# Gate weights of experts 20 and 27 loaded in six and five transfers of spaced rows instead of one

## The chip, the cores and the metric

The kernel runs on one core of a Trainium2 chip. The metric is the time of one execution on the device, in microseconds (us). The time before is the median of three runs; beside it stands one profiled execution, whose trace is read here. "Us" with two decimals after a row is a time from the start of the span of that execution, or a duration.

## What is computed

The reference is one decoder block over 256 tokens of width 1024 with 16 meta tokens ahead of them: an RMSNorm, a combined input projection, a pooling mixer and a gated DeltaNet, an output projection, and then a mixture of 32 experts in four groups, of which each token uses the two best of its best group. The expert part is what matters here:

```python
for gi in range(N_EXPERT_GROUPS):
    hdn = (jax.nn.silu(jnp.einsum('nd,edf->nef', xt, w_gate[gi]))
           * jnp.einsum('nd,edf->nef', xt, w_up[gi]))
    hdn = hdn * comb[:, gi, :, None].astype(hdn.dtype)
    y = y + jnp.einsum('nef,efd->nd', hdn, w_down[gi])
```

`w_gate` and `w_up` of an expert are 1024x512 and `w_down` is 512x1024, in float32: 2 MiB each, 6 MiB for an expert, 192 MiB for all 32. They are read from HBM once.

## The kernel before, in words

The front half (mixers and output projection) takes the first 300 us or so. There the first expert's weights are loaded in twelve transfers of 32 rows (L768), between the tiles of the input projection, and expert 1's gate and up in four transfers of columns each (L792).

The back half goes through the experts e = 0 to 31 in order. For each, TensorE does gate (L2143, c = 0, 32 records of the trace), up (L2143 again, c = 1, 32 more), parts of the gather of the next group of four experts (L2075, only while e < 28), turns of the hidden state (L2175, L2181), every second expert the spreading of results to tokens (L2154), and down (L2199). VectorE multiplies gate and up (L1697); ScalarE takes the gate's bank with silu (L1076) and copies (L1081, L1092).

The weights lie in `ring`, nine places of 16 KiB in each of the 128 partitions: three matrices (gate c = 0, up c = 1, down c = 2) of three experts (`RINGS = 3`, expert e uses places of e % 3). One matrix is one transfer: `dst` is a place of the ring over all 128 partitions, `src` is a contiguous 2 MiB block of HBM whose 128 rows of 16 KiB go to one partition each. `load_chunk` issues it from SyncE's queue (SP), in the order gate, up, down, expert after expert. Before expert e's gate is loaded, SP waits until expert e - 3's gate has been used (semaphores `gate`, `up`, `y`); nothing else holds a load back. So up to nine loads are queued or under way. The last expert's up is cut into two transfers of columns and its down into four (L709), each with a semaphore of its own.

When a transfer is complete, its semaphore `w_land...` stands 16 higher; TensorE waits in `landed(e, c)` until the semaphore of the place has the count that all loads into the place up to this one add up to. A transfer more therefore needs a count of 16 more.

Of the kernel before, what the change touches and what calls it, by code (L numbers as in the profile page):

```python
# [40 lines left out]
P = 128  # L41
# [33 lines left out]
RINGS = 3  # L75
# [12 lines left out]
SEEDS_AT = {0: [2], 1: [3]}  # L88
FIRST_BANK = [5, 4, 7, 6]
YS = 2 * EXPERTS - 1  # L90
WARM = 16
BRIDGE = 4
KQV = 4
# [321 lines left out]
def uses(n, k, slots):  # L415

    return (n - k + slots - 1) // slots


def build_block(nc, x, meta_tokens, norm_mix_w, w_in, conv_w, pool_w, pool_scale, a_log, dt_bias, dn_norm_w,  # L420
# [3 lines left out]
    with ctx:  # L424
# [16 lines left out]
        S = Named()  # L441
# [259 lines left out]
        def load_chunk(eng, e, c):  # L701

            dst = ring[:, RING_AT[3 * (e % RINGS) + c], :]
            src = (gate_v, up_v, down_v)[c][e]
            if e == EXPERTS - 1 and c:
                parts, name = ((2, "last_up_land"), (4, "last_down_land"))[c - 1]
                dst2, src2 = (v.rearrange("p (s m) -> p s m", s=parts) for v in (dst, src))
                for n in range(parts):
                    eng.dma_start(dst2[:, n, :], src2[:, n, :]).then_inc(S(f"{name}{n}"), 16)  # L709
            else:  # L710
                eng.dma_start(dst, src).then_inc(S(f"w_land{3 * (e % RINGS) + c}"), 16)

# [18 lines left out]
        def _(sp):  # L731
# [28 lines left out]
            for step in SEQ_OF["sp"]:  # L760
# [32 lines left out]
                if step[0] == "early":  # L793
                    if step[1] == 0:
                        filled(sp, ("oT", HEADS - 1))
                    else:
                        low_made(sp, len(TILES) + KT - 1)
                        low_made(sp, len(TILES) + KT - 2)
                    load_chunk(sp, 2, step[1])
            sp.wait_ge(S("outproj"), 3)  # L800

            def one_pass(ps):
                base = EXPERTS * ps
                again = not isinstance(ps, int)
                for e in range(EXPERTS):
                    if e == RINGS and not again:

                        sp.wait_ge(S("logits"), TT)
                        sp.dma_start(wfin, norm_final_w[None, :].to_broadcast([P, D])).then_inc(S("wf_land"), 16)
                    for c, used in enumerate(("gate", "up", "y")):  # L810
                        if e >= RINGS:
                            sp.wait_ge(S(used), base + (e - RINGS + 1))
                        elif again:
                            sp.wait_ge(S(used), base)
                        if again or (e and (e, c) not in EARLY):
                            load_chunk(sp, e, c)
# [15 lines left out]
        def _(act):  # L832
# [231 lines left out]
            def one_pass(ps):  # L1064
# [3 lines left out]
                for e in range(EXPERTS):  # L1068
# [25 lines left out]
                    if g == 1 and not last:  # L1094

                        act.wait_ge(S("ysb"), YS * ps + 2 * e + 2)
                        act.wait_ge(S("give"), PAIRS * ps + (pair + 1))
# [670 lines left out]
        def _(pe):  # L1768
            T = nc.tensor
            pe.wait_ge(S("consts"), CONSTS["ones"])  # L1770
            for _ in range(WARM):
                T.matmul(pb[6][:, 384:384 + P], ones[:], ones[:], start=True, stop=True)
# [74 lines left out]
            for step in SEQ_OF["pe"]:  # L1847
                kind = step[0]
                if kind == "abp":
                    k = step[1]  # L1850
# [19 lines left out]
                if kind == "proj":  # L1870
                    n, k = step[1:]
# [72 lines left out]
                if kind == "sb":  # L1944
                    h, c = step[1:]
# [13 lines left out]
                if kind == "sa":  # L1959
                    h, c = step[1:]  # L1960
# [19 lines left out]
                if kind == "outk":  # L1980
                    k, i = step[1:]
# [5 lines left out]
                    for kk, half in which:  # L1987
                        if kk == 0:
                            bank(pe, ("out", 2 * i + half))
                        n = len(TILES) + kk  # L1990
# [30 lines left out]
            for n in range(TT * KT + 3):  # L2021
                if n >= 3:
                    cast_off(n - 3)
                if n < TT * KT:
                    k, i = n % KT, n // KT
# [34 lines left out]
            def one_pass(ps):  # L2060
# [49 lines left out]
                def landed(e, c):  # L2110

                    short = c and e % RINGS == (EXPERTS - 1) % RINGS
                    if e == 0 and not again:
                        pe.wait_ge(S(f"first_land{c}"), 4 * 16)
                        return
                    loads = ps * (uses(EXPERTS, e % RINGS, RINGS) - short) - (e % RINGS == 0)
                    quarters = QUARTERS - 1 if e % RINGS == 1 and c < 2 else 0
                    pe.wait_ge(S(f"w_land{3 * (e % RINGS) + c}"), 16 * (loads + quarters + (e // RINGS + 1)))

                def gate_up(e, c, name):  # L2120

                    q, j, i, g = e // 4, e % 4, e // 2, e % 2
                    first = e == 0 and not again
                    if not first and c == 0:
                        pe.wait_ge(S("xgT"), parts + PARTS * (q + 1) - 2)
                    if not (c == 1 and e == EXPERTS - 1):
                        landed(e, c)
                    if not first:
                        pe.wait_ge(S("hmid"), experts + e)
                        if c == 0:  # L2130
                            pe.wait_ge(S("hT"), experts + e)
                        elif g == 0:
                            pe.wait_ge(S("give"), pairs + i)
                    w = ring[:, RING_AT[3 * (e % RINGS) + c], :].rearrange("p (k q h j) -> p k h q j", k=KT, h=2, j=2)
                    for kt in range(KT):
                        if first and c == 0 and kt % 4 == 0:
                            pe.wait_ge(S("xgT_side"), kt // 4 * 2 + 2)
                        if first and c == 0 and kt % 4 == 2:
                            pe.wait_ge(S("xgT"), kt // 4 + 1)
                        if c == 1 and e == EXPERTS - 1 and kt % (KT // 2) == 0:  # L2140
                            pe.wait_ge(S(f"last_up_land{kt // (KT // 2)}"), 16 * ps + 16)
                        for half in range(2):
                            ins = T.matmul(pb[5 + c][half * 64:half * 64 + SLOTS, 0:256], xgT[:, q % ROOMS, kt, j * SLOTS:(j + 1) * SLOTS],  # L2143
                                           w[:, kt, half], start=(kt == 0), stop=(kt == KT - 1), skip_group_check=True)
                    ins.then_inc(S(name), 1)
# [12 lines left out]
                def spread_last():  # L2158

                    pe.wait_ge(S("give"), pairs + PAIRS)  # L2160
                    pe.wait_ge(S("ysb"), YS * (ps + 1))
                    for t in range(TT):
# [20 lines left out]
                def down(e):  # L2183

                    pe.wait_ge(S("hT"), experts + (e + 1))
                    if e == 0 and not again:
                        pe.wait_ge(S("most"), 1)
                    if again or e:
                        pe.wait_ge(S("ysb"), YS * ps + 2 * e)
                    if again and e == 0:  # L2190
                        pe.wait_ge(S("ysb_side"), 1 * ps)
                    if e < EXPERTS - 1:
                        landed(e, 2)
                    w = ring[:, RING_AT[3 * (e % RINGS) + 2], :].rearrange("p (j d) -> p j d", j=4)
                    for j in range(4):
                        if e == EXPERTS - 1:
                            pe.wait_ge(S(f"last_down_land{j}"), 16 * ps + 16)
                        for half in range(2):
                            ins = T.matmul(pb[7][half * 64:half * 64 + SLOTS, :], hT[:, j % 2, j // 2 * SLOTS:(j // 2 + 1) * SLOTS], w[:, j, half * 512:(half + 1) * 512],  # L2199
                                           start=(j == 0), stop=(j == 3), skip_group_check=True)  # L2200
                    ins.then_inc(S("y"), 1)
# [66 lines left out]
```

## Time and profile before

| | us |
|---|---|
| median of 3 runs | 781.25 (780.7 to 785.59) |
| the profiled execution, its own time | 781.17 |
| its span, first to last instruction | 779.4 |
| TensorE busy (749.0 us) | 96% of the span |
| DMA, mean over the span | 309 GB/s |

What lies between the span and the time of the profiled execution is 1.77 us. A busy TensorE says little by itself, since the ends of matmuls are modelled; which of TensorE's starts was held back by what is read from the waits, and how busy the 16 DMA engines were from the DMA share, the mean busy share of these engines.

### The profile page before, as it was taken

The numbers are of one execution on the slowest core, as the hardware profiler recorded it, in microseconds if no ns is written. First come the engines' busy times: TensorE is split into PE (matmuls) and PEld (weight loads), VectorE is DVE, ScalarE is ACT, GpSimd is POOL, SyncE is SP. The second block draws the span as 40 slices with busy tenths as digits, with TensorE's granted clock in tenths as the row PEclk, the third lists the DMA queues.
The fourth block names the chain that finished last, engine by engine and source line by source line (L and its number), as shares of the span: only waits on it lengthen the run. The fifth ranks groups of instructions, "written<-read, shape, count | busy, mean of one in ns | idle before, by whom it ended". The sixth has DMA issues, their size and how long they took to land.

```text
span 779.4 us, 16087 instructions
## 1 busy us (share of the span) xinstructions
PE 749.0 (96%) x6517; PEld 535.0 (69%) x6517; DVE 323.2 (41%) x794; ACT 312.1 (40%) x632; POOL 124.6 (16%) x208
## 2 busy tenths in 40 slices
PE   8999999999999999899999999999999988998895
PEld 7989989998999988655655555555556555455452
DVE  4784787688575855811311211221113112112012
ACT  6876678576684744712221221212122211111113
POOL 7473242225433640000000000000000000000000
PEclk9999999999999999999999999999999999999999
DMA  8537555564754568999999999999999999999992
GB/s 205 145 85 183 154 143 130 136 150 114 186 137 125 160 192 320 375 380 430 428 426 428 426 428 430 425 427 425 430 427 427 427 427 425 428 430 426 427 409 96
DMA packets 81104, 241.06 MB, mean 309 GB/s; under 512 B 6913, under 2 KB 65394, under 8 KB 68994
## 3 DMA queue, kind: packets, MB, share of 16 engines
q1 hardware_dynamic: 80722, 239.19, 80.7%
q8 instruction: 54, 0.88, 0.5%
q10 hardware_dynamic: 304, 0.79, 0.4%
q14 instruction: 24, 0.20, 0.1%
HBM read 238.92 MB, written 1.05 MB: 308 GB/s over the span
## 4 chain that ended last, share of the span: by engine, by line
PE 75%; DMA 11%; DVE 6%; issue 5%; POOL 2%; ACT 1%; DVEq 0%; POOLq 0%; ACTq 0%
PE banks L2143 23%; PE banks L1798 18%; PE banks L2199 12%; DMA ring<-in_expert_w_up_dram 10%; PE banks L2075 3%; PE banks L2154 3%; PE banks L1993 2%; PE banks L2175 1%; DVE desk L1367 1%; PE banks L1930 1%; PE banks L1917 1%; DVE rounded L1316 1%; PE banks L1934 1%; PE banks L1955 1%; PE banks L1978 1%
## 5 line engine op out<-in xcount | busy, mean ns | idle before, releaser
L2143 PE MATMUL banks<-ring,bench 128*64 128x256 f32 x2048 | 240.0, 388 | 11.6 <-DMA ring<-in_expert_w_up_dram 7.7
L2143 PEld LDWEIGHTS banks<-ring,bench 128*64 128x64 f32 x2048 | 146.2, 134 | 112.8 <-issue 23.1
L1798 PE MATMUL banks<-rounded 128*128 128x256 f32 (+3 forms) x1344 | 197.5, 293 | 1.4 <-DVE rounded L1328 1.0
L1798 PEld LDWEIGHTS banks<-rounded 128*128 128x128 f32 (+1 forms) x1344 | 170.1, 187 | 5.4 <-POOL rounded L1192 1.2
L1697 DVE TENSOR_TENSOR bench<-banks,bench 128x256 f32<-128x256 f32 x32 | 13.6, 425 | 263.0 <-PE banks L2143 172.1
L2199 PE MATMUL banks<-ring,bench 128*64 128x512 f32 x512 | 116.9, 598 | 0.5 <-ACT bench L1081 0.5
L1092 ACT ACTIVATE ysb<-banks 64x512 f32<-64x512 f32 x63 | 37.2, 591 | 147.1 <-PE banks L2199 146.3
L2199 PEld LDWEIGHTS banks<-ring,bench 128*64 128x64 f32 x512 | 33.9, 136 | 63.2 <-issue 60.1
L860 ACT ACTIVATE rounded<-room 128x1024 fp32r<-128x1024 f32 x64 | 67.4, 1054 | 22.5 <-PE banks L1798 15.0
L1081 ACT ACTIVATE bench<-banks 128x256 f32<-128x256 f32 x32 | 12.3, 384 | 148.1 <-PE banks L2175 148.1
L1316 DVE TENSOR_TENSOR rounded<-room,rounded 128x1024 fp32r<-128x1024 f32 x49 | 61.2, 1249 | 15.4 <-ACT rounded L860 14.3
L1185 POOL TENSOR_TENSOR rounded<-room,rounded 128x256 fp32r<-128x256 f32 x60 | 43.8, 760 | 60.4 <-ACT rounded L860 60.3
L1667 DVE SCALAR_TENSOR_TENSOR ylo<-ysb,bench,yhi 128x512 fp32r<-128x512 f32 x30 | 21.2, 749 | 65.5 <-ACT yhi L1099 65.5
L1367 DVE SCALAR_TENSOR_TENSOR desk<-banks,prmT,desk 128x271 f32<-128x271 f32 (+5 forms) x72 | 35.3, 491 | 5.1 <-ACT desk L870 3.0
L1076 ACT ACTIVATE bench<-banks 128x256 f32<-128x256 f32 x32 | 12.3, 384 | 60.0 <-PE banks L2143 60.0
L2075 PE MATMUL banks<-hot,xhi 128*128 128x256 f32 x112 | 34.9, 334 | 0.0
L1658 DVE TENSOR_TENSOR bench<-banks,gain 128x512 f32<-128x512 f32 x30 | 20.7, 692 | 20.7 <-PE banks L2075 18.7
L2075 PE MATMUL banks<-hot,xlo 128*128 128x256 f32 x112 | 28.9, 280 | 0.0
L2075 PEld LDWEIGHTS banks<-hot,xhi 128*128 128x128 f32 x112 | 21.1, 188 | 11.0 <-issue 11.0
L2154 PE MATMUL banks<-yhi,give 128*128 128x512 f32 x60 | 23.7, 395 | 0.0
L2154 PE MATMUL banks<-ylo,give 128*128 128x512 f32 x60 | 23.5, 392 | 0.0
L2075 PEld LDWEIGHTS banks<-hot,xlo 128*128 128x128 f32 x112 | 21.3, 190 | 0.5 <-issue 0.5
(309 smaller groups left out, 858.3 us busy)
## 6 DMA issues: line engine op xcount, KB each, us to landing
ring<-in_expert_w_gate_dram SPq DMA_DIRECT2D x30, 2048.0 KB, 29.0
ring<-in_expert_w_down_dram SPq DMA_DIRECT2D x30, 2048.0 KB, 27.8
ring<-in_expert_w_up_dram SPq DMA_DIRECT2D x29, 2048.0 KB, 29.2
room<-in_w_in_dram SPq DMA_DIRECT2D x56, 512.0 KB, 4.4
ring<-in_expert_w_gate_dram SPq DMA_DIRECT2D x8, 512.0 KB, 5.9
ring<-in_expert_w_up_dram SPq DMA_DIRECT2D x8, 512.0 KB, 6.5
ring<-in_expert_w_down_dram SPq DMA_DIRECT2D x8, 512.0 KB, 18.3
room<-in_w_out_dram SPq DMA_DIRECT2D x8, 512.0 KB, 4.4
```

The costliest lines, as they stand in the source:

```text
L860: nc.scalar.activation(whi[:, n % HI_SLOTS], win[:, n % WIN_SLOTS].rearrange("p k c -> p (k c)"), ACT.Copy).then_inc(S("whi"), 1)
L1092: nc.scalar.activation(ysb[g * SLOTS:(g + 1) * SLOTS, half * 512:(half + 1) * 512], pb[7][half * 64:half * 64 + SLOTS, :], ACT.Copy).then_ ...
L1185: ins = nc.gpsimd.tensor_tensor(wlo[:, lo_slot(n), cols], w[:, cols], whi[:, n % HI_SLOTS, cols].bitcast(F32), ALU.subtract)
L1316: V.tensor_tensor(wlo[:, lo_slot(n)], w, whi[:, n % HI_SLOTS].bitcast(F32), ALU.subtract).then_inc(S("wlo"), 1)
L1367: ins = V.scalar_tensor_tensor(acc[:, i, f + sh:L], p[:, 0:L - f - sh], prmT[:, tap * 24 + col:tap * 24 + col + 1], acc[:, i, f + sh:L], A ...
L1658: V.tensor_tensor(xgT[:, q % ROOMS, per * part:per * (part + 1), :], pb[FIRST_BANK[part] if q == 0 and not again else 4][:].rearrange("p ( ...
L1667: V.scalar_tensor_tensor(ylo[:, cols], ysb[:, cols], wslot[:, 0:1], yhi[:, cols].bitcast(F32), ALU.mult, ALU.subtract).then_inc(S("ylo"), 1)
L1798: ins = T.matmul(o, a, b[:, k, lo_at:L], start=(k == 0 and n == 0), stop=(k == KT - 1 and n == 2))
L2075: ins = T.matmul(pb[4][:, k * WIDE:(k + 1) * WIDE], x[:, t, ch:ch + P], hot[:, t, :], start=(t == 0 and x is xhi), stop=(t == TT - 1 and x ...
L2143: ins = T.matmul(pb[5 + c][half * 64:half * 64 + SLOTS, 0:256], xgT[:, q % ROOMS, kt, j * SLOTS:(j + 1) * SLOTS], w[:, kt, half], start=(k ...
L2154: ins = T.matmul(pb[2 * t + half], give[:, t * P:(t + 1) * P], y[:, half * 512:(half + 1) * 512], start=False, stop=True, skip_group_check ...
L2199: ins = T.matmul(pb[7][half * 64:half * 64 + SLOTS, :], hT[:, j % 2, j // 2 * SLOTS:(j // 2 + 1) * SLOTS], w[:, j, half * 512:(half + 1) * ...
```

## The change

`SPLIT` names two of the 96 loads: the gate (c = 0) of expert 20 and of expert 27. Each is issued as several transfers of the same 128 rows of 16 KiB, all with the semaphore of the place. For expert 20: the 64 even rows; the 32 rows 1, 5, 9, ...; and four transfers of eight rows, 3, 19, 35, ..., then 7, 23, ..., then 11, 27, ..., then 15, 31, .... For expert 27: the 64 even rows; the 32 rows 1, 5, 9, ...; the 16 rows 3, 11, 19, ...; and two transfers of eight rows, 7, 23, ... and 15, 31, .... The bytes and their places are the same. `landed` adds 16 for each transfer more, from that expert on, for the users of the same place.

```diff
+SPLIT = {(20, 0): (slice(0, P, 2), slice(1, P, 4)) + tuple(slice(r, P, 16) for r in (3, 7, 11, 15)),
+         (27, 0): (slice(0, P, 2), slice(1, P, 4), slice(3, P, 8)) + tuple(slice(r, P, 16) for r in (7, 15))}
...
+            elif (e, c) in SPLIT:
+                for rows in SPLIT[e, c]:
+                    eng.dma_start(dst[rows], src[rows]).then_inc(S(f"w_land{3 * (e % RINGS) + c}"), 16)
             else:
                 eng.dma_start(dst, src).then_inc(S(f"w_land{3 * (e % RINGS) + c}"), 16)
...
-                    pe.wait_ge(S(f"w_land{3 * (e % RINGS) + c}"), 16 * (loads + quarters + (e // RINGS + 1)))
+                    split = 0
+                    for (n, k), rows in SPLIT.items():
+                        if (n % RINGS, k) == (e % RINGS, c):
+                            split += (len(rows) - 1) * (ps + (1 if n <= e else 0))
+                    pe.wait_ge(S(f"w_land{3 * (e % RINGS) + c}"), 16 * (loads + quarters + split + (e // RINGS + 1)))
```

## Rows read from the trace of the kernel before

**Rows 1.** The page, its slices, each a fortieth of the span.
```profile
PE   8999999999999999899999999999999988998895
...
PEclk9999999999999999999999999999999999999999
DMA  8537555564754568999999999999999999999992
...
DMA packets 81104, 241.06 MB, mean 309 GB/s; under 512 B 6913, under 2 KB 65394, under 8 KB 68994
```

**Rows 2.** DMA queues from 345 to 740 us: packets, MB, share of 16 engines.
```profile
q1 hardware_dynamic: 11556, 168.27, 100.2%
q8 instruction: 22, 0.36, 0.4%
```

**Rows 3.** TensorE's waits, 600 us to the end: total, times, longest.
```profile
PE banks L2143 <- DMA ring<-in_expert_w_up_dram: 7.7, 9, 1.3
PE banks L2143 <- issue: 3.8, 5, 0.9
```

**Rows 4.** TensorE's waits from 330 to 600 us, all there are.
```profile
PE banks L2175 <- DVE bench L1697: 0.3, 1, 0.3
```

**Rows 5.** TensorE in order of time: starts, durations, idle before.
```profile
593.69 6.51 PE L2143 MATMUL banks<-ring,bench 128*64 128x256 f32 x56
...
626.12 3.84 PE L2143 MATMUL banks<-ring,bench 128*64 128x256 f32 x32 [1.02 <-DMA ring<-in_expert_w_up_dram]
...
745.02 3.84 PE L2143 MATMUL banks<-ring,bench 128*64 128x256 f32 x32 [1.01 <-DMA ring<-in_expert_w_up_dram]
...
755.14 7.42 PE L2143 MATMUL banks<-ring,bench 128*64 128x256 f32 x64
...
764.05 3.65 PE L2199 MATMUL banks<-ring,bench 128*64 128x512 f32 x16 [0.26 <-ACT bench L1081]
```

**Rows 6.** SP's issues: start, duration; the gates of experts 20 and 27 first.
```profile
558.26 0.33 SPq L711 DMA_DIRECT2D ring<-in_expert_w_gate_dram  x1
...
655.39 0.33 SPq L711 DMA_DIRECT2D ring<-in_expert_w_gate_dram  x1
660.52 0.33 SPq L711 DMA_DIRECT2D ring<-in_expert_w_up_dram  x1
...
714.67 0.33 SPq L711 DMA_DIRECT2D ring<-in_expert_w_gate_dram  x1
```

**Rows 7.** From issue to landing: gate 20, then gate 31.
```profile
DMA to landing us min/median/max: 33.5/33.5/33.5
...
DMA to landing us min/median/max: 40.2/40.2/40.2
```

**Rows 8.** Windows at the end of the loads: stretch, engines, PEclk, DMA share, GB/s.
```profile
758.00:758.50 0.50, 0.50 (x8) 0.28 (x4) 0.00 (x0) 0.00 (x0) 0.00 (x0) 1.00 0.95 385
758.50:759.00 0.50, 0.50 (x8) 0.29 (x5) 0.00 (x0) 0.02 (x1) 0.00 (x0) 1.00 0.89 360
...
760.50:761.00 0.50, 0.50 (x8) 0.28 (x4) 0.00 (x0) 0.00 (x0) 0.00 (x0) 1.00 0.56 229
761.00:761.50 0.50, 0.50 (x8) 0.29 (x6) 0.00 (x0) 0.00 (x0) 0.00 (x0) 1.00 0.50 205
...
763.00:763.50 0.50, 0.36 (x3) 0.36 (x4) 0.08 (x1) 0.00 (x0) 0.00 (x0) 1.00 0.40 164
763.50:764.00 0.50, 0.30 (x3) 0.06 (x1) 0.17 (x1) 0.38 (x1) 0.00 (x0) 1.00 0.22 90
764.00:764.50 0.50, 0.45 (x2) 0.20 (x4) 0.26 (x1) 0.48 (x1) 0.00 (x0) 1.00 0.06 25
```

**Rows 9.** Windows: a 32-row load alone; four 64-row loads of x; the full loads.
```profile
73.50:74.50 1.00, 1.00 (x11) 1.00 (x10) 1.00 (x2) 0.98 (x3) 0.00 (x0) 1.00 0.98 213
...
3.50:5.50 2.00, 2.00 (x12) 2.00 (x11) 0.55 (x2) 1.35 (x4) 1.45 (x7) 1.00 1.02 229
...
620.00:740.00 120.00, 108.20 (x748) 59.95 (x744) 20.18 (x48) 21.53 (x42) 0.00 (x0) 1.00 1.01 427
```

**Rows 10.** Window in which the six smaller last loads were moved.
```profile
750.00:757.00 7.00, 7.00 (x42) 3.49 (x42) 0.28 (x2) 1.49 (x3) 0.00 (x0) 1.00 1.00 414
```

**Rows 11.** SP's issues of smaller transfers: 32 rows; 8 rows twice.
```profile
57.28 0.58 SPq L768 DMA_DIRECT2D ring<-in_expert_w_gate_dram  x1
...
3.12 0.37 SPq L738 DMA_DIRECT2D room<-in_norm_mix_w_dram  x1
3.53 0.27 SPq L738 DMA_DIRECT2D room<-in_pool_scale_dram  x1
```

## Prediction

> **What bounds the kernel now.** I read the page's slices first [rows 1]. TensorE shows 9 nearly everywhere at full clock, and from about 310 us on the DMA line shows 9 as well: both are candidates. The waits tell them apart. From 330 to 600 us TensorE waited once, 0.3 us, for VectorE [rows 4]: it set the pace and the loads were ahead. From 600 us on it waited nine times for a load, 7.7 us in all, and 3.8 us more before L2143 with no releaser named [rows 3]; in the timeline these fall on the starts of gates, the other half of the same pattern. So the loads decide from about 620 us. TensorE's starts confirm it: the ups of experts 22 and 30 both began right behind a load, at 626.12 and 745.02 us [rows 5]. Between them lie eight experts, 24 loads, in 118.90 us, or 4.95 us a load. The last gate to matter, expert 31's, was issued at 714.67 and landed 40.2 us later, at 754.9 [rows 6, 7], and TensorE took it at 755.14. Behind it nothing waits for a load any more.
>
> The rate says what limits a load: 427 GB/s with a DMA share of 1.01 over these 120 us [rows 9]. 2.097 MB at 427 GB/s are 4.91 us, so all 16 engines are busy all the time. Each moves 8 of the 128 rows, 0.61 us a row. That one row is one packet follows from the page: of 81104 packets 12110 are of 8 KB or more [rows 1], and the 192 MiB of expert weights are 12288 rows.
>
> **The engines don't finish together**, and this is what the change can touch. Every engine has its own backlog, and a load has landed when the last engine has done its rows. The windows at the end show the backlogs [rows 8]. With no more work queued, the share times 16 is the number of engines still at work: 15.2 at 758.0 to 758.5, 14.2 next, 9.0 at 760.5 to 761.0, 8.0 at 761.0 to 761.5, 6.4 at 763.0 to 763.5, 3.5 in the next half, 1.0 in the last. The first engine is through about 758.7, eight are by 761.2, and the other half goes on until 763 to 764.4. The latest is some 5.7 us behind the first. The drift has a source in the trace: while all engines were full, 22 fetches of instructions of 16 KB each (0.36 MB) went over the same engines [rows 2], each to one of them, and an engine that is always full never makes that up. Six smaller ones at the end fit the 4.95 against 4.91 us above: the slowest engine lost 24 x 0.04 = 1.0 us between 626 and 745 us.
>
> **Part 1: rows change engines.** A load of 128, 64, 32 or 16 rows gives every engine the same number. A row is one packet, so a transfer of eight rows can occupy eight engines at most. Expert 20 has four of these: eight engines get 4 + 2 + 4 = 10 rows if they are the same eight every time, the others 4 + 2 = 6, where each had 8. Expert 27 has two: 4 + 2 + 1 + 2 = 9 against 7. In sum three rows, 3 x 0.61 = 1.84 us, are added to the backlog of eight engines and taken off that of the other eight. The backlog never drains before the end, so both stay. Which eight take the rows no row of this trace tells. The Trainium skill ("DMA: Bandwidth & Descriptors", Why a DMA increments its semaphore by 16 and not by 1) says that a transfer issued from SP that can't use all engines goes to the lowest-numbered ones; rows here neither show a number of an engine nor which numbers are late.
>
> If the eight early ones take them, the last early engine goes from about 761.2 to 763.0 us and the last late one from 764.4 to 762.6. The last load is then complete at 763.0 instead of 764.4: 1.4 us earlier, and so are the loads of experts 28 to 31, those of 21 to 27 by up to 1.2 us. TensorE can use it: from the up of expert 30 (745.02) it worked without a load's wait to 755.14, 10.1 us; started 1.4 us earlier it gets there at 753.7, and gate 31 is in at 754.9 - 1.4 = 753.5. From there to the end the work is the same: expert 31's down at 764.05 [rows 5] moves with it. The term is -1.4 us, between 0 and -1.84 (the whole shift).
>
> **Part 2: the pieces themselves.** Nine transfers more. SP issues a 32-row one in 0.58 us, 8-row ones in 0.37 and 0.27 us, against 0.33 us now [rows 6, 11]: about 2.3 us for expert 20 and 2.1 for 27, where SP has 3.6 and 5.1 us until its next issue, and the load lands 33.5 us after issue [rows 7]. Cost 0; without that backlog it would be these 2 us each. Behind SP's longer issue stands only its next load. On the engines a further transfer means a completion more and a seam: the window with the smaller last loads moved 414 GB/s against 427, 3% of 7 us over some five transfers, 0.04 us each [rows 9, 10]. Nine make 0.4 us; I take 0.3, between 0 and 0.4. Waits gain no instruction, only a higher count. Gate 20 itself lands at 558.26 + 33.5 = 591.8 and is wanted at 593.69 [rows 5]: 1.9 us of room, enough for two rows more.
>
> **Part 3: where the spaced rows are written.** The trace has no spaced rows, but it has loads that are not of 128 partitions. The 32-row load ran at 213 GB/s with a share of 0.98, and the four 64-row loads of x at 229 GB/s with a share of 1.02 [rows 9]: engines busy all the time at half the rate, 1.2 us for a row of 16 KB. Those go to 32 or 64 neighbouring partitions. Spaced rows reach the whole height like the full loads do (0.61 us), and 13 to 19 rows an engine are affected, so the bounds are 0 and 0.61 us for each of them. I take 0, since the set of partitions is that of the full load; the other end is the rival below.
>
> **Sum.** -1.4 + 0.3 = -1.1 us against the profiled execution's 781.17: 780.1 us. It agrees with the median of the runs within 0.1, so nothing is added.
>
> **The rivals.** *Shared write paths (slower).* If half the rate in part 3 comes from two engines writing to the same part of the memory, then an engine whose spaced rows leave its usual partitions meets that part's usual owner, and both go at half rate. The eight engines with the extra rows have 10 + 9 = 19 such rows; all doubled cost 11.6 us. With half of them doubled, as engines at different backlogs meet only partly, the last early engine ends at 761.2 + 1.84 + 5.8 = 768.8, 4.4 us after the present end: 785.6. All doubled: 774.6, 791.4 us. The rival decides as soon as the early engines lose the 1.4 us that separate 763.0 from 764.4, that is with 2.3 doubled rows of 19. For it speaks that both half-rate rows are plain; against it that they all used one half or quarter of the partitions.
> The Trainium skill ("SBUF — State Buffer", Door 1: The DMA port swizzle) gives this as a rule: partitions share 16 ports of about 27 GB/s by bits of their number, and 32 or 64 neighbours reach only eight. The trace's 213 and 229 GB/s agree. By its formula the eight rows 16 apart fall on four ports.
>
> *The wrong eight (slower).* The extra rows go to the eight late engines: 764.4 + 1.84 = 766.2, all loads up to 1.84 us later, 781.17 + 1.84 = 783.0. For it: nothing in the rows orders the engines. Against: nothing either; that the fetches run on queue 8 is a slim hint that the upper eight serve it, and I lean on no more.
>
> *No shift.* The 8-row transfers go round the engines, or the late ones are mixed among both groups: 781.2 to 781.9 with the seams of part 2.
>
> **Chances.** Early eight at full rate 0.44 (780.1, own range 779.2 to 781.2); shared write paths 0.28 (782 to 791); wrong eight 0.18 (782.5 to 784); no shift 0.10. About 1% of 781 us, 7.8 us, is what a measurement of this kernel can tell from no change. Faster than 773.4 needs more than all backlog differences together: 0.01. Slower than 789.1 needs more than three quarters of the rows doubled: 0.07. The rest, 0.92, is within. The range leaves out the far end of the shared paths above 787.5, about 0.1, and below 778.8, where the whole shift (779.3) and half a microsecond of scatter lie.
>
> **What would show it.** In the windows from 758 us on, the share falls over some 4.5 us instead of 5.7, and the last engine ends near 763; TensorE's waits before L2143 shrink from 11.5 by about 1 us; gate 31 lands near 753.5. With shared paths the GB/s dips clearly below 427 around 585 to 600 and 688 to 700 us, and the loads behind land some us later. With the wrong eight there is no dip, but the share's fall stretches to over 7 us. The prediction is wrong if the spaced rows are slow or the late engines take them; those are its two unseen quantities.

## The result, and the profile after

The changed kernel takes 792.44 us (median of 6 runs, 789.54 to 795.26) against 781.93 us (6 runs) before, in the same session: ratio 1.0126, 95% interval 1.0102 to 1.0149. By the medians it is slower by 10.5 us, by the ratio (which comes from the single runs) by 9.9, between 8.0 and 11.7 us; 1.1 us less was forecast, and the time lies above the range. The profiled execution was the fastest of the six: 789.54 us with a span of 787.8 us, 8.4 us longer than that of before. It is these 8.4 us that the traces can explain. One execution of the run with even and odd rows took 1417 us and enters no ratio.

The page of the changed kernel, its slices of 19.7 us each, beside [rows 1]:

```profile
DMA  8437564456664559999999999999999999999991
GB/s 210 136 96 186 136 161 133 118 142 156 141 162 122 152 179 379 367 408 429 428 427 427 428 428 426 425 428 427 429 378 392 427 426 428 429 341 426 426 404 77
...
DMA packets 81200, 241.06 MB, mean 306 GB/s; under 512 B 7009, under 2 KB 65490, under 8 KB 69090
```

The DMA line still shows 9 throughout, but the GB/s under it fall twice, to 378 and 392 and later to 341. A busy share alone would hide this. The dips lie where the prediction looked for them under shared write paths (around 585 to 600 and 688 to 700 us). The windows around the two split loads (stretch, the engines' busy time, PEclk, DMA share, GB/s), first of the changed kernel:

```profile
585.00:595.00 10.00, 8.59 (x58) 4.30 (x54) 1.78 (x4) 1.79 (x5) 0.00 (x0) 1.00 1.01 267
595.00:690.00 95.00, 87.12 (x602) 50.22 (x602) 18.36 (x42) 17.32 (x33) 0.00 (x0) 0.98 1.01 428
690.00:706.00 16.00, 12.01 (x75) 6.73 (x77) 2.01 (x6) 1.57 (x3) 0.00 (x0) 0.98 1.01 320
```

and of the kernel before, where nothing happens there:

```profile
585.00:595.00 10.00, 10.00 (x72) 5.48 (x70) 1.78 (x4) 1.83 (x4) 0.00 (x0) 1.00 1.00 424
...
690.00:706.00 16.00, 15.66 (x109) 9.26 (x109) 2.38 (x7) 2.32 (x5) 0.00 (x0) 1.00 1.01 428
```

With a share of 1.01 at 267 GB/s all 16 engines are at work on rows that take 0.61 x 427 / 267 = 0.98 us. Expressed as time at the full 427 GB/s, the bytes not moved in the first dip cost 10 x (427 - 267) / 427 = 3.7 us, the second 16 x (427 - 320) / 427 = 4.0 us. Between the dips and behind them the rate is as before [rows 9]. 3.7 + 4.0 = 7.7 us of the 8.4 us are there. That no engine was spared shows at the end of the loads: from 764 to 765 us the share is still 0.99 (windows further down), while before the last engine was through at 764.4.

They arrive at the end undiminished. TensorE in order of time, with its idle time before and what ended it, to be read beside [rows 5]:

```profile
595.90 9.07 PE L2152 MATMUL banks<-ring,bench 128*64 128x256 f32 x64 [2.31 <-issue]
...
704.76 9.07 PE L2152 MATMUL banks<-ring,bench 128*64 128x256 f32 x64 [3.84 <-issue]
...
753.40 3.84 PE L2152 MATMUL banks<-ring,bench 128*64 128x256 f32 x32 [1.03 <-DMA ring<-in_expert_w_up_dram]
...
763.53 7.42 PE L2152 MATMUL banks<-ring,bench 128*64 128x256 f32 x64
772.44 3.65 PE L2208 MATMUL banks<-ring,bench 128*64 128x512 f32 x16 [0.26 <-ACT bench L1086]
```

The first two are the gates of experts 20 and 27, for which TensorE now waits 2.31 and 3.84 us ("issue" means that no releaser is named, as in [rows 3]); gate 20 starts 2.2 us later than its 593.69 of before. Expert 30's up starts 8.4 us later than at 745.02, expert 31's gate and down 8.4 us later than at 755.14 and 764.05, and the rest is unchanged.

### The profile page after: what moved, and what is told of

It is laid out like the page before. It is cut to its first block, busy times and chain, and to the rows that moved or that the text cites. A ratio compares the mean times of both kernels' runs of the same rounds, so it can differ in the third digit from the quotient of the medians.

```text
span 787.8 us, 16096 instructions
## 1 busy us (share of the span) xinstructions
PE 751.8 (95%) x6517; PEld 538.4 (68%) x6517; DVE 323.2 (41%) x794; ACT 312.3 (40%) x632; POOL 124.8 (16%) x208
## 4 chain that ended last, share of the span: by engine, by line
PE 74%; DMA 11%; DVE 6%; issue 5%; POOL 1%; ACT 1%; DVEq 0%; POOLq 0%; ACTq 0%
PE banks L2152 23%; PE banks L1803 18%; PE banks L2208 12%; DMA ring<-in_expert_w_up_dram 10%; PE banks L2080 3%; PE banks L2163 3%; PE banks L1998 2%; PE banks L2184 1%; DVE desk L1372 1%; PE banks L1935 1%; PE banks L1922 1%; DVE rounded L1321 1%; PE banks L1939 1%; PE banks L1960 1%; PE banks L1983 1%
## 5 line engine op out<-in xcount | busy, mean ns | idle before, releaser
L2152 PE MATMUL banks<-ring,bench 128*64 128x256 f32 x2048 | 243.0, 392 | 17.0 <-issue 10.5
L2152 PEld LDWEIGHTS banks<-ring,bench 128*64 128x64 f32 x2048 | 150.0, 136 | 117.7 <-issue 30.0
L2208 PEld LDWEIGHTS banks<-ring,bench 128*64 128x64 f32 x512 | 33.9, 136 | 63.2 <-issue 60.1
L1663 DVE TENSOR_TENSOR bench<-banks,gain 128x512 f32<-128x512 f32 x30 | 20.8, 692 | 20.6 <-PE banks L2080 18.7
## 6 DMA issues: line engine op xcount, KB each, us to landing
ring<-in_expert_w_down_dram SPq DMA_DIRECT2D x8, 512.0 KB, 19.7
```

Of the source, the lines that this page charges most:

```text
L1663: V.tensor_tensor(xgT[:, q % ROOMS, per * part:per * (part + 1), :], pb[FIRST_BANK[part] if q == 0 and not again else 4][:].rearrange("p ( ...
```

## The experiments

All times are medians, with the ratio to the kernel before on the same chip and its 95% interval. Two questions were open: which part of the splits is slow, and where the late engines are. The diffs are shortened to the lines that matter. They are against the changed kernel, those of the extra transfers against the kernel before. In the runs an entry of `SPLIT` also names the columns (all of them but in the run with columns), and the kernels with extra transfers wait for the last of them before the output is stored.

**Even and odd rows.** Spaced rows without small transfers.

```diff
+SPLIT = {k: (slice(0, P, 2), slice(1, P, 2)) for k in ((20, 0), (27, 0))}
```

> Gates of experts 20 and 27 in two transfers each, even rows and odd rows: every engine keeps its 8 rows, no transfer of eight rows is left. Shared write paths: spaced rows alone are slow; the changed kernel moved about 265 GB/s instead of 427 in its dips, so each split load of 4.9 us takes some 3 us more: 4 to 7 us above before (786 to 789 us), with two dips in the GB/s. Wrong eight engines: no shift here, so 782 us, as before. Cost of more transfers: two more, 782 us.

Measured: 781.91 us, ratio 0.9995 (0.9974 to 1.0016). No dip: 428 GB/s in both windows. 64 rows two apart cost nothing. Shared paths, in the form in which every spaced row pays, were wrong.

**Columns.** The same number of transfers, none spaced.

```diff
+CUTS = {20: (0, 2048, 3072, 3328, 3584, 3840, 4096), 27: (0, 2048, 3072, 3584, 3840, 4096)}
...
-                    eng.dma_start(dst[rows], src[rows])
+                    eng.dma_start(dst[:, a:b], src[:, a:b])      # a, b: neighbours in CUTS[e]
```

> Six and five transfers as in the change, of the same sizes, but cut by columns over all 128 partitions: the same number of issues and completions, no spaced rows, no shift. Shared write paths: 782 to 782.5 us. Cost of more transfers (issue, completion, seam): the whole loss of the change comes back, 790 us or more. Wrong eight: 782 us.

Measured: 783.4 us, ratio 1.0018 (0.9997 to 1.0038), no dip like the change's (418 and 423 GB/s, 0.6 us in all). Nine more issues and completions are not the loss.

**Eights 4 apart, and eights side by side,** for expert 20 alone.

```diff
+SPLIT = {(20, 0): [slice(s + r, s + 32, 4) for s in (0, 32) for r in range(4)] + [slice(64, P)]}   # 4 apart
+SPLIT = {(20, 0): [slice(8 * r, 8 * r + 8) for r in range(8)] + [slice(64, P)]}                    # side by side
```

> Gate of expert 20 alone: partitions 0 to 63 in eight transfers of eight rows 4 apart (0, 4, ..., 28; 1, 5, ...), partitions 64 to 127 in one of 64 rows. Eight engines move 12 rows, the others 4. Shared write paths: if engine i writes partitions 4i to 4i + 3 in a full load too, the eights cost nothing; the 64-row one runs at half rate (4 rows more of 0.61 us, 2.4 us), and the shift of four rows adds up to 2.4 us to the eight engines: 0 to 5 us above before, 782 to 787 us. Wrong eight: 2.4 us above before plus the half rate, 787 us. This run is the partner of the next; their difference counts.

> As the run with the eights 4 apart, but the eights are neighbouring partitions (0 to 7, 8 to 15, ...): the same count, the same engines, the same bytes, only other partitions per transfer. Shared write paths: eight engines write to two groups of partitions at a time, a quarter of the rate, 8 rows at 2.4 instead of 0.61 us: 7 to 15 us above the partner. Wrong eight and cost of transfers: the same time as the partner.

Measured: 793.15 us (ratio 1.0131, 1.0082 to 1.0179) and 795.9 us (1.0165, 1.0119 to 1.0211). One split expert loses as much as the two of the change. Both expectations failed: the run with eights 4 apart was to lose 5 us at most and lost 10.2 (6.4 to 14.0) by the ratio, and the pair doesn't separate, 2.8 us instead of 7 to 15, within the intervals of each other. Their stretches around gate 20, 4 apart and then side by side, are equally slow:

```profile
575.00:615.00 40.00, 29.71 (x194) 16.87 (x190) 5.87 (x14) 5.23 (x10) 0.00 (x0) 0.83 1.01 314
```

```profile
575.00:615.00 40.00, 28.52 (x188) 16.34 (x185) 5.87 (x14) 5.02 (x10) 0.00 (x0) 0.87 1.01 315
```

That is 40 x (427 - 314) / 427 = 10.6 us in the one and 10.5 in the other. Both share the transfer of partitions 64 to 127, which is slow itself, as the run with halves shows below. The pair was badly chosen, since it held a slow part constant. But that part doesn't explain the sum either: see the halves.

**No eights,** and **sixteens.** The change's 64 and 32 rows, with the rest in 32 rows, or in two transfers of 16 rows 8 apart.

```diff
+SPLIT = {k: (slice(0, P, 2), slice(1, P, 4), slice(3, P, 4)) for k in ((20, 0), (27, 0))}                    # no eights
+SPLIT = {k: (slice(0, P, 2), slice(1, P, 4), slice(3, P, 8), slice(7, P, 8)) for k in ((20, 0), (27, 0))}    # sixteens
```

> Gates of experts 20 and 27 in three transfers: 64 even rows, rows 1, 5, 9, ..., rows 3, 7, 11, .... No transfer of eight rows, no shift of rows between engines. Even and odd rows alone cost nothing (781.9 us), so two causes are left. Eights: only transfers of eight rows are slow, 782 us here and no dip of the GB/s. Small spacing: every spaced transfer of fewer than 64 rows is slow for where it writes, so the 64 rows left to them cost at least what they did in the change: 788 to 793 us.

> Both gates in four transfers: 64, 32, 16 and 16 spaced rows (the two sixteens 8 apart). The last sixteen is what the change cuts into two eights for expert 27. Every engine keeps 8 rows. Eights: 782 us. Small spacing: 788 to 793 us. If only this one of the two runs without eights is slow, it is the sixteens.

Measured: without eights 781.47 us (ratio 0.9993, 0.9968 to 1.0018); with sixteens 789.61 us (1.0081, 1.0053 to 1.011). The windows of the run with 32-row transfers, then of the one with sixteens:

```profile
585.00:595.00 10.00, 10.00 (x84) 6.20 (x82) 0.92 (x2) 1.95 (x4) 0.00 (x0) 1.00 1.01 428
690.00:706.00 16.00, 15.56 (x108) 8.84 (x110) 2.01 (x6) 1.95 (x4) 0.00 (x0) 1.00 1.00 426
```

```profile
585.00:595.00 10.00, 10.00 (x78) 5.85 (x76) 1.78 (x4) 0.82 (x3) 0.00 (x0) 1.00 1.03 318
690.00:706.00 16.00, 11.70 (x75) 6.18 (x71) 2.00 (x6) 1.95 (x4) 0.00 (x0) 0.96 1.02 313
```

So eight rows, or eight engines, aren't the condition: sixteen rows 8 apart, one for each engine, are as bad (7.9 us lost in their dips from 575 to 615 and 685 to 730 us, and 7.9 in those of the change over the same windows), and 32 rows 4 apart are free. The change has 32 rows per expert in transfers of 16 or 8 rows (4 x 8 for expert 20, 16 + 2 x 8 for expert 27), the sixteens have 32 too. The dips of the change come to 3.7 x 16 / 32 = 1.9 and 4.0 x 16 / 32 = 2.0 us of one engine for each such row, on top of the 0.61 us of the row itself.

**Neighbouring rows in the source.** Read or written?

```diff
-                    eng.dma_start(dst[rows], src[rows])
+                    eng.dma_start(dst[rows], src[take])      # eights: take = eight neighbouring rows
```

> The change with the same transfers to the same partitions, but each transfer of eight reads eight neighbouring rows of the weights instead of rows 16 apart; so some rows of the two gates hold other weights than they should. Reading: if the distance in the source is what slows them, the loss goes, 782 us (with the rest of the shift between 780 and 784). Writing or the number of engines: 790 to 793 us as in the change.

Measured: 792.82 us, ratio 1.0131 (1.0086 to 1.0176), with dips to 333 and 350 GB/s in the same windows. They are less deep there but reach further: from 595 to 605 us the rate is still 352 GB/s, and in all (575 to 615 and 685 to 730 us) they cost 7.6 us, where those of the change cost 7.9. So the distance between the eight rows in the source is nothing. The edit leaves the places that are written as they were, and what remains is the side that is written, by elimination.

**Extra transfers of eight rows, 4 apart, 16 apart, side by side.** The kernel before, with the loads whole, and sixteen small transfers of 4 KB rows beside them.

```diff
...
+                            if e in (20, 27) and c == 0 and not again:
+                                if e == 27:
+                                    sp.wait_ge(S("extra_land"), 8 * 16)
+                                for rows in EIGHTS:
+                                    sp.dma_start(spare[rows, D:2 * D], gate_v[0][rows, 0:D]).then_inc(S("extra_land"), 16)
# EIGHTS: slice(s + r, s + 32, 4) for s in (0, 32), r < 4;  or slice(r, P, 16) for r < 8;  or slice(8 * r, 8 * r + 8) for r < 8
```

> The kernel before, with eight more transfers of eight rows of 4 KB behind the gate of expert 20 and eight more behind that of expert 27, into room that is free then: 1.25 us more for each of eight engines, twice, partitions 0 to 63 in steps of four. Nothing of the loads is split. If the eight engines are the early ones, and an eight costs only its bytes, the end stays within 0.5 us of before; if they are the late ones, 2.5 us more, 784.5. Eights that slow all engines whatever they carry: 785 us and more, with two dips of the GB/s.

> As the run with eight extra transfers of eight rows of 4 KB behind gates 20 and 27 (784.7 us, no dip), with the same bytes, counts and eight engines, but rows 16 apart over all 128 partitions instead of 4 apart in one quarter. Shared write paths: the eight rows fall on fewer write paths than engines, and engines that meet there slow the rest as well; the split loads cost about 2 us of one engine for each such row of 16 KB, so 128 rows of 4 KB cost some 4 us on every engine: 787 to 789 us, with dips. Only the number of engines or of rows counts: 784.7, as the partner.

> The same again with eight neighbouring partitions in each extra transfer (0 to 7, 8 to 15, ...). Shared write paths: still fewer paths for the eight rows than 16 apart gives, so at least as slow as that: 787 to 792 us. Distance between the rows as such is the cause: 784.7 us, since neighbours are the smallest distance.

Measured: 784.68 us (ratio 1.003, 1.0004 to 1.0056), 789.33 us (1.0111, 1.0094 to 1.0129) and 787.29 us (1.0093, 1.0067 to 1.0119). The 10 us around the landing of gate 20 and of the transfers behind it, in this order:

```profile
585.00:595.00 10.00, 10.00 (x73) 5.45 (x71) 1.78 (x4) 1.68 (x4) 0.00 (x0) 1.00 1.00 424
```

```profile
585.00:595.00 10.00, 9.23 (x64) 4.88 (x62) 1.78 (x4) 2.05 (x4) 0.00 (x0) 1.00 1.01 313
```

```profile
585.00:595.00 10.00, 10.00 (x72) 5.62 (x70) 1.78 (x4) 1.89 (x4) 0.00 (x0) 1.00 1.02 347
```

This is the pair that the eights of expert 20 should have been: the same engines, counts and bytes, only other partitions. Four apart there is no dip, 16 apart and side by side there is: 5.3 and 4.3 us lost in the two stretches together. Side by side was expected to be at least as slow as 16 apart and is not (347 against 313 GB/s), so the order among those that lose is not explained. Nor do these runs, with rows of 4 KB, say that eights 4 apart are free for rows of 16 KB.

The same run with eights 4 apart answers the second question. Its windows at the end of the loads, beside [rows 8]:

```profile
761.00:762.00 1.00, 1.00 (x12) 0.61 (x10) 0.00 (x0) 0.29 (x1) 0.00 (x0) 1.00 0.67 274
762.00:763.00 1.00, 1.00 (x12) 0.64 (x10) 0.00 (x0) 0.09 (x1) 0.00 (x0) 1.00 0.59 242
763.00:764.00 1.00, 1.00 (x14) 0.57 (x10) 0.00 (x0) 0.00 (x0) 0.00 (x0) 1.00 0.32 131
764.00:765.00 1.00, 1.00 (x12) 0.54 (x8) 0.00 (x0) 0.00 (x0) 0.00 (x0) 1.00 0.16 66
765.00:766.00 1.00, 0.41 (x5) 0.13 (x2) 0.42 (x1) 0.00 (x0) 0.00 (x0) 1.00 0.09 37
766.00:767.00 1.00, 0.75 (x6) 0.48 (x8) 0.42 (x1) 0.64 (x2) 0.00 (x0) 1.00 0.05 20
```

Eight engines carry 2.5 us more here. Were they the late half, which before worked on until 763 to 764.4, some seven would still be at work from 764 to 765; 0.16 x 16 = 2.6 are. Were they the early half, the last engine would still end at 764.4; it ends after 766. So the eight that take such transfers are some late and some early ones, with one of the latest among them. (This takes it that the same engines are late in both executions, which the traces can't show.)

**Halves.** Neighbouring rows, every engine with 8 rows.

```diff
+SPLIT = {k: (slice(0, 64), slice(64, P)) for k in ((20, 0), (27, 0))}
```

> Both gates in two transfers of 64 neighbouring rows, partitions 0 to 63 and 64 to 127; every engine keeps 8 rows, four in each, no row is far from the next. Shared write paths: 16 engines write to one half of the partitions, at half the rate or worse as in the 32- and 64-row loads of the kernel before, twice 5 us or more: 792 us and above, two dips. One row per engine in a transfer is the cause, not the place: 782 us, like even and odd rows.

Measured: 799.73 us, ratio 1.0246 (1.0229 to 1.0264), the slowest of all, with 218 GB/s over the 10 us:

```profile
585.00:595.00 10.00, 8.52 (x62) 4.98 (x60) 1.78 (x4) 0.77 (x2) 0.00 (x0) 1.00 0.98 218
595.00:605.00 10.00, 4.76 (x25) 2.50 (x22) 2.08 (x4) 2.52 (x4) 0.00 (x0) 0.66 0.99 334
```

Two transfers, no small one, no shift: the place alone does it, and the rate is the half rate of the 64-row loads in [rows 9]. But it costs more than half rate for 2 MB would, which is 4.7 us for each gate: the dips take 7.6 us at gate 20 and 9.7 at gate 27. Why is not shown. Of the 10.6 and 10.5 us of the two runs with expert 20 in eights, which have one such half and not two, this accounts for about 4 us, if a half costs half of 7.6. The other 6.7 us or so belong to the eights of 16 KB rows, or to what they do beside the half, and they are there even for the eights 4 apart.

**Experts 8 and 15** instead of 20 and 27, where TensorE set the pace.

```diff
-SPLIT = {(20, 0): ..., (27, 0): ...}
+SPLIT = {(8, 0): ..., (15, 0): ...}      # the same slices
```

> The change's two splits at experts 8 and 15 instead of 20 and 27. There TensorE sets the pace and the loads are some us ahead. If the engines' queues never run dry from 345 us on, 8 us lost there are missing at the end all the same: 789 to 793 us, as in the change. If the lead of the loads hides them: 782 us.

Measured: 791.62 us, ratio 1.0144 (1.0107 to 1.0181). The dips are at 410 to 420 and 515 to 530 us, 7.2 us in all. TensorE works on through both, waits for a load for the first time shortly before 533 us instead of from 620 on, and the loss is there at the end:

```profile
412.00:420.00 8.00, 8.00 (x54) 4.89 (x52) 2.01 (x6) 0.38 (x1) 0.00 (x0) 1.00 1.00 281
```

**The losses side by side.** Each run has one profiled execution, and these differ before anything of the change begins. SP's issue of expert 15's down, in the kernel before, the changed kernel and the one with sixteens:

```profile
501.20 0.33 SPq L711 DMA_DIRECT2D ring<-in_expert_w_down_dram  x1
```

```profile
500.92 0.33 SPq L716 DMA_DIRECT2D ring<-in_expert_w_down_dram  x1
```

```profile
503.69 0.33 SPq L715 DMA_DIRECT2D ring<-in_expert_w_down_dram  x1
```

TensorE sets the pace there, and the issue follows it. With this offset taken off the difference of the spans, what is left comes from the back half. The dips are the time lost against 427 GB/s from 575 to 615 and 685 to 730 us (for experts 8 and 15 from 400 to 430 and 505 to 535 us); the last column is what eight engines have to carry more, at 0.61 us for 16 KB. All in us:

| run | span longer | offset | left | dips | rows more |
|---|---|---|---|---|---|
| the change | 8.4 | -0.3 | 8.7 | 7.9 | 1.8 |
| neighbouring rows in the source | 12.1 | 3.0 | 9.1 | 7.6 | 1.8 |
| experts 8 and 15 | 9.8 | 0.8 | 9.0 | 7.2 | 1.8 |
| sixteens | 10.0 | 2.5 | 7.5 | 7.9 | 0 |
| no eights | 3.9 | 4.2 | -0.3 | -0.1 | 0 |
| even and odd | 2.1 | 1.4 | 0.7 | 0.1 | 0 |
| columns | 0.6 | 0.0 | 0.6 | 0.6 | 0 |
| extra, 4 apart | 2.8 | 0.2 | 2.6 | 0.2 | 2.5 |
| extra, 16 apart | 7.6 | -0.6 | 8.2 | 5.3 | 2.5 |
| extra, side by side | 6.2 | -0.5 | 6.7 | 4.3 | 2.5 |
| halves | 18.7 | 0.5 | 18.2 | 17.3 | 0 |
| expert 20, 4 apart | 15.1 | 2.9 | 12.2 | 10.8 | 2.4 |
| expert 20, side by side | 17.4 | 4.0 | 13.4 | 10.4 | 2.4 |

Dips and rows more add up to what is left within 1.0 us in every run. So the loss at the end has these two parts, also for expert 20 in eights; open is why its dip is so deep.

## Why the prediction was wrong, point by point

*What bounds the kernel: right.* The loads decide from 620 us, all engines are always full, and what is lost there is lost at the end. The run with experts 8 and 15 shows it more sharply than the prediction said: even where TensorE sets the pace and waits for nothing, a loss of rate costs its full length (7.2 us in the dips, 9.0 at the end, of which up to 1.8 for the rows that change engines).

*Part 3, where the spaced rows are written: the step that failed.* "I take 0, since the set of partitions is that of the full load." The set over all transfers is that of the full load, but the set of each transfer isn't, and that is what counts. Where a shape was tried by itself, slow are 64 neighbours, 16 rows 8 apart, 8 rows 16 apart and 8 neighbours; free are 64 rows 2 apart, 32 rows 4 apart, and 8 rows 4 apart (these last with rows of 4 KB only). So the term put at 0 measured 3.7 + 4.0 = 7.7 us. The runs don't give a rule with a price: eights 4 apart with rows of 16 KB, beside a transfer of 64 neighbours, belong to a stretch that lost 10.6 us, and the half in it accounts for about 4.
The Trainium skill ("SBUF — State Buffer", Door 1: The DMA port swizzle) sorts these seven the same way by its formula for the 16 ports. Worked out with it, the slow transfers reach 8, 8, 4 and 2 ports, fewer than the 16, 16, 8 and 8 engines that can take part, and the free ones 16, 16 and 8, as many as engines. The traces agree in all seven, with 218 to 347 GB/s around gate 20 for the slow shapes and 424 to 428 for the free shapes. They don't agree in the order (2 ports lose less than 4) nor for expert 20 in eights 4 apart, which by the formula reach a port for each engine. Ports at which engines meet are the page's account; the runs show that the choice of partitions in a transfer decides, and no run shows the ports themselves.

*The rival of shared write paths was the right one, with the wrong count.* It doubled the spaced rows of the eight engines with extra rows and came to 785.6 us for half of them, 791.4 us for all. Of its 19 rows for each of eight engines most were free: the 64- and 32-row transfers, 12 of them. Those of the 16- and 8-row transfers, 64 rows in all, cost 1.9 to 2.0 us each, not 0.61, because in a dip all 16 engines slow down, and a row takes 0.98 us on average. The price came near 791.4 by two errors that cancel. The point from which the rival decides (1.4 us lost) was far exceeded. That it had 0.28 was the judgement that failed: the two half-rate rows in [rows 9] were set aside because they used one part of the partitions, without asking which part each transfer of eight reaches.

*Part 1, rows change engines: the mechanism holds, its sign didn't.* The -1.4 us needed the extra rows to go to the early half. The run with extra eights shows the late engines mixed among both groups, with a latest one in the group that takes the rows. This was the case put down as no shift; here it does add: that run lost 2.7 us (784.68 against 781.94; by the ratio 2.3, between 0.3 and 4.4) for 2.5 us more on eight engines, so "no shift" put at 0 a term that a single late engine in the group makes positive. The end of the loads of the changed kernel, its fall of the share, shows the same:

```profile
764.00:765.00 1.00, 1.00 (x12) 0.66 (x10) 0.00 (x0) 0.93 (x2) 0.00 (x0) 1.00 0.99 401
...
769.00:770.00 1.00, 1.00 (x12) 0.66 (x10) 0.00 (x0) 0.00 (x0) 0.00 (x0) 1.00 0.26 107
...
772.00:773.00 1.00, 0.74 (x6) 0.28 (x6) 0.42 (x1) 0.98 (x2) 0.00 (x0) 1.00 0.05 20
```

Engines drop out from 765 to 773 us, over some 8 us, where 4.5 were forecast and 5.7 measured before; over 7 us was the sign named for the wrong eight. How much it cost the changed kernel is only roughly shown. The three kernels with these slow rows and three rows more on eight engines have 8.7, 9.1 and 9.0 us left in the table, the one with sixteens, as slow and without such rows, 7.5: 1.2 to 1.6 us more, of 1.84 possible, where -1.4 were forecast. Each is one execution. That late engines come from fetches of instructions was argued from [rows 2] and tested by no run.

*Part 2, the pieces.* The 0.3 us stand as far as they can be told: the run with columns has 1.4 us (-0.2 to 3.0). SP's issues took longer than forecast, 3.67 us for six and 3.05 us for five instead of 2.3 and 2.1, and cost nothing: the six began at 557.99 us, and the next issue came at 561.71 us, where the kernel before has 561.88.

Slower than 789.1 us had 0.07, for a rival whose own bounds reached 791.4. The range ended at 787.5 by leaving out just the end at which the result lies. What stays open: why eight neighbours lose less than eight rows 16 apart, why a half costs more than its half rate, and why expert 20 in eights 4 apart plus 64 neighbours loses more than 64 neighbours' share of the run with halves.

## What to carry to other kernels

When a load is split, check the partitions of each single transfer, not of their sum. Here 64 rows 2 apart and 32 rows 4 apart over all 128 partitions kept the full rate; fewer rows further apart, and neighbours, didn't. Shapes that were not tried have to be measured, with whole rows and between the loads that surround them. Where a queue of loads is never empty, a lower rate costs its full length at the end, wherever it occurs in that stretch, and even if nobody waits for it then. And a DMA share of 1 says only that the engines are occupied: read the GB/s beside it. Before the spans of two single traces are compared, a mark ahead of the change should be compared: here it lay up to 4.2 us apart.

## What the runs showed of the hardware that was not expected

A few badly placed rows slow all 16 engines: 64 rows of 16 KB in small transfers cost the 16 engines 7.7 us each, some 1.9 us of one engine for each row whose own transfer is 0.61 us. Eight extra transfers of eight 4 KB rows, 2 MB x 1/8 in all, brought the rate from 424 to 313 GB/s over 10 us when their rows were 16 apart and left it alone when they were 4 apart.

TensorE's clock fell after its waits: idle for 2.31 us before gate 20, then granted 0.50 of full speed, its level of 1.2 GHz, from 596.5 to 599 us, and 1.00, 2.4 GHz, again from 600 us on. The next 64 matmuls took 9.07 us instead of 7.42.

```profile
596.50:599.00 2.50, 2.50 (x14) 1.73 (x12) 1.29 (x3) 0.00 (x0) 0.00 (x0) 0.50 1.03 439
```

It did the same after the 3.84 us before gate 27. The loads went on at 428 GB/s from 595 to 690 us all the while, so nothing of the 8.4 us is put down to it.
